# LoRA's products of a two-layer RWKV, conv, MoBA and RetNet trunk: four 32-row tiles or four products over 96 stacked rows

## What is computed

```python
p = p + (token_shift(p) - p) * mu
r, k, v, wl, al = jnp.split(p, [G, 2 * G, 3 * G, 3 * G + L], axis=-1)   # G = 256, L = 32
decay = jnp.exp(-RWKV_DECAY_SCALE * jax.nn.sigmoid(w0 + jnp.tanh(wl) @ w2))
a = jax.nn.sigmoid(a0 + al @ a2)
kk = kk / jnp.maximum(jnp.sqrt(jnp.sum(kk * kk, axis=-1, keepdims=True)), 1e-12)
...
bonus = jnp.sum(rh * kh * r_k.astype(jnp.float32), axis=-1, keepdims=True) * vh
```

## Time and profile before

| | us |
|---|---|
| median of three runs (range) | 576.95 (575.99 to 576.97) |
| the profiled execution: its time | 576.78 |
| its span | 575.0 |
| around the span | 1.78 |

### The profile page before, as it was taken

How to read it: one execution, slowest core, us unless ns; L and a number is a source line. 1 busy time by engine, 2 the same in 40 slices (tenths; PEclk the granted TensorE clock), 3 DMA queues, 4 the chain that set the end, 5 groups by cost and what they waited for, 6 DMA issues and landing times. The chain is left out here.

```text
span 575.0 us, 12739 instructions
## 1 busy us (share of the span) xinstructions
PE 567.4 (99%) x5244; PEld 464.0 (81%) x5244; DVE 381.0 (66%) x644; ACT 278.3 (48%) x555; POOL 249.3 (43%) x197
## 2 busy tenths in 40 slices
PE   9999999999999999999999999999999999999995
PEld 7978888888877777888898788888888777788884
DVE  4999976482488557774543897947537865778163
ACT  5486231343574475534656743324357335735253
POOL 4946552044941323536335455402386313145340
PEclk9999999999999999999999999999999999999998
DMA  9546634056432122353535423332743321224513
GB/s 281 161 130 206 212 97 111 8 130 149 109 79 75 39 75 62 113 171 132 165 117 139 111 77 108 88 70 58 161 127 83 77 73 39 73 75 147 184 40 143
DMA packets 103373, 64.58 MB, mean 112 GB/s; under 512 B 29151, under 2 KB 94227, under 8 KB 103316
## 3 DMA queue, kind: packets, MB, share of 16 engines
q1 hardware_dynamic: 103316, 63.77, 39.4%
HBM read 55.61 MB, written 8.14 MB: 111 GB/s over the span
## 5 line engine op out<-in xcount | busy, mean ns | idle before, releaser
L706 POOL TENSOR_TENSOR w_lo<-w_raw,w_hi 128x512 fp32r<-128x512 f32 x156 | 216.6, 1409 | 283.0 <-ACT w_hi L1295 277.7
L772 PE MATMUL bank<-act_hi,w_hi 128*128 128x512 f32 x432 | 173.2, 401 | 0.0
L775 PE MATMUL bank<-act_lo,w_hi 128*128 128x512 f32 x432 | 168.5, 390 | 0.0
L774 PE MATMUL bank<-act_hi,w_lo 128*128 128x512 f32 x416 | 162.3, 390 | 0.0
L1295 ACT ACTIVATE w_hi<-w_raw 128x512 fp32r<-128x512 f32 x140 | 80.3, 622 | 74.1 <-PE bank L857 28.2
L772 PEld LDWEIGHTS bank<-act_hi,w_hi 128*128 128x128 f32 x432 | 81.1, 188 | 24.7 <-issue 8.2
L775 PEld LDWEIGHTS bank<-act_lo,w_hi 128*128 128x128 f32 x432 | 81.1, 188 | 17.4
L774 PEld LDWEIGHTS bank<-act_hi,w_lo 128*128 128x128 f32 x416 | 78.2, 188 | 14.8
L1221 PE MATMUL bank<-w_hi,act_hi 128*128 128x512 f32 x128 | 50.0, 390 | 0.0
L1223 PE MATMUL bank<-w_hi,act_lo 128*128 128x512 f32 x128 | 49.8, 389 | 0.0
L1222 PE MATMUL bank<-w_lo,act_hi 128*128 128x512 f32 x128 | 49.8, 389 | 0.0
(11 more groups left out here) (217 smaller groups left out, 961.0 us busy)
## 6 DMA issues: line engine op xcount, KB each, us to landing
w_raw<-in_w_in_dram SPq DMA_DIRECT2D x62, 512.0 KB, 4.1
w_raw<-in_w_out_dram SPq DMA_DIRECT2D x16, 512.0 KB, 3.8
pages<-in_x_dram SPq DMA_DIRECT2D x4, 512.0 KB, 6.3
x_or_y<-in_x_dram SPq DMA_DIRECT2D x4, 512.0 KB, 4.2
x_scratch<-x_or_y SPq DMA_DIRECT2D x4, 512.0 KB, 2.9
x_or_y<-x_scratch SPq DMA_DIRECT2D x4, 512.0 KB, 3.7
out_dram<-pages SPq DMA_DIRECT2D x8, 256.0 KB, 2.2
bias_scratch<-pages SPq DMA_DIRECT2D x1, 1280.0 KB, 8.1
```

Source lines behind the costliest of these rows:

```text
L706: ins = pool.tensor_tensor(low, raw, w_hi[:, i % HI, k, 0:n].bitcast(F32), ALU.subtract)
L772: mm(b[:, :], hi, act_hi[:, k, :], start=n == 0, stop=False)
L774: mm(b[:, :], lo, act_hi[:, k, :], start=False, stop=False)
L775: ins = mm(b[:, :], hi, act_lo[:, k, :], start=False, stop=n == KT - 1)
```

## The change

LoRA's products take 96 rows: rows 0 to 31 the high part of the weight, rows 32 to 63 its low part, rows 64 to 95 the high part again, against the input's high part twice and its low part. One float32r product of 96 rows then holds all three terms. The weights are loaded raw three times, ACT copies them all and DVE subtracts for the 32 rows of the low part, in layer 0 only. ACT makes the input's high parts (four copies of 32 rows, one Tanh), and DVE two low parts in a new step `lora_low`, ahead of the scaling that is split off `kk_unit` as `kk_scale`. On PE the products come behind v0 instead of ahead of it. The split of the bonus input becomes a step `rkv_parts` behind the copy of rq0, and bonus's products move behind rk0. At the start six filler products go, and DVE waits for the norm's spread products one at a time, ahead of the first two scalings.

```diff
-          ("kk_norm",), ("kk_unit", 0), ("lora_tanh",), ("shift", "r1"), ("kk_unit", 1), ("lora",), ("shift", "v0"), ("decay_scan",), ("shift", "v1"),
+          ("kk_norm",), ("kk_unit", 0), ("lora_tanh",), ("lora_low",), ("shift", "r1"), ("kk_scale", 0), ("kk_unit", 1), ("kk_scale", 1), ("shift", "v0"), ("lora",), ("decay_scan",), ("shift", "v1"),
...
-    s += [("copy", "rq0"), ("copy", "rq1"), ("bonus",), ("rotate", "rq0"),
-          ("copy", "rk0"), ("rotate", "rq1"), ("scores", 0), ("scores", 1), ("copy", "rk1"), ("rotate", "rk0"), ("to_rows", "v"), ("scores", 2),
+    s += [("copy", "rq0"), ("rkv_parts",), ("copy", "rq1"), ("rotate", "rq0"),
+          ("copy", "rk0"), ("rotate", "rq1"), ("bonus",), ("scores", 0), ("scores", 1), ("copy", "rk1"), ("rotate", "rk0"), ("to_rows", "v"), ("scores", 2),
...
-            for p in range(2):
-                for r, w in ((2 * p, rwkv_w2), (2 * p + 1, rwkv_a2)):
-                    load(lora_w[r * LORA:(r + 1) * LORA], w[:, :, p * P:(p + 1) * P].rearrange("l k c -> k l c"), "const_b")
+            for r in range(3):
+                for z, w in enumerate((rwkv_w2, rwkv_a2)):
+                    load(lora_raw[r * LORA:(r + 1) * LORA, z], w.rearrange("l k c -> k l c"), "lora_loaded")
...
-            idle(3)
             pe.wait_ge(s("const_a"), 16)
             turn(0, 0)
             turn(1, 0)
-            idle(4)
+            idle(1)
...
                 def lora():
-                    pe.wait_ge(*at("lora_in", layer))
-                    for p in range(2):
-                        for z, r0 in (("zw", 2 * p * LORA), ("za", (2 * p + 1) * LORA)):
-                            b = begin(f"{z}{p}", layer)
-                            end(mm(b[:, :], lora_w[r0:r0 + LORA, layer, :], WA[r0:r0 + LORA, :], start=True, stop=True, tile_position=(r0, 0)), f"{z}{p}", layer)
+                    if layer == 0:
+                        pe.wait_ge(s("lora_weight"), 2)
+                    for p in range(2):
+                        for z, name in enumerate(("zw", "za")):
+                            pe.wait_ge(*at("lora_in", layer, 2 - z))
+                            b = begin(f"{name}{p}", layer)
+                            end(mm(b[:, :], lora_w[:, z, layer, p * P:(p + 1) * P], stat_hi[0:3 * LORA, z, :], start=True, stop=True), f"{name}{p}", layer)
...
+                    if layer == 0:
+                        act.wait_ge(s("lora_loaded"), 16 * 6)
+                        go(lora_w.rearrange("p z l c -> p (z l c)"), lora_raw.rearrange("p z l c -> p (z l c)"), ACT.Copy).then_inc(s("lora_weight"), 1)
...
-                    go(WA[2 * LORA:4 * LORA], WA[0:2 * LORA], ACT.Copy).then_inc(s("lora_copied"), 1)
-                    act.wait_ge(*at("lora_copied", layer))
-                    for r0 in (0, 2 * LORA):
-                        go(WA[r0:r0 + LORA], WA[r0:r0 + LORA], ACT.Tanh).then_inc(s("lora_in"), 1)
+                    go(WA[0:LORA], WA[0:LORA], ACT.Tanh).then_inc(s("lora_bent"), 1)
+                    for z in (1, 0):
+                        if z == 0:
+                            act.wait_ge(*at("lora_bent", layer))
+                        for r in range(2):
+                            go(stat_hi[r * LORA:(r + 1) * LORA, z, :], WA[z * LORA:(z + 1) * LORA], ACT.Copy).then_inc(s("lora_high"), 1)
...
             dve.memset(bias_rows[:, :, T:DIST], MASKED)
-            for a in range(2):
-                dve.wait_ge(*full(f"nw{a}", -1))
             for two in (0, 2):
                 for t in (two, two + 1):
                     invert_root(t, 0)
                     for a in range(2):
+                        if t == 0:
+                            dve.wait_ge(*full(f"nw{a}", -1))
...
                         if layer == 0:
+                            dve.wait_ge(s("lora_weight"), 1)
+                            low = slice(LORA, 2 * LORA)
+                            tt(lora_w[low], lora_raw[low], lora_w[low].bitcast(F32), ALU.subtract).then_inc(s("lora_weight"), 1)
                             bias_runs(3)
...
+
+                def kk_scale(p):
                     stt(KN[:, p, :], K[:, p, :], par[:, layer, KKP + p:KKP + p + 1], KN[:, p, :], ALU.mult, ALU.mult).then_inc(s("kk_unit"), 1)
+
+                def lora_low():
+                    for z in (1, 0):
+                        dve.wait_ge(*at("lora_high", layer, 4 - 2 * z))
+                        r = slice(z * LORA, (z + 1) * LORA)
+                        tt(stat_hi[2 * LORA:3 * LORA, z, :], WA[r], stat_hi[r, z, :].bitcast(F32), ALU.subtract).then_inc(s("lora_in"), 1)
```

## The result

The changed kernel takes 579.12 us (median of six runs, 578.87 to 579.3), the kernel before 576.88 (six runs, 575.99 to 577.3). The ratio is 1.0037, 95% interval 1.0027 to 1.0048: slower by 2.2 us, where 578.2 and slower was forecast, with a range of 576.0 to 580.0. The profiled execution took 578.87, with a span of 577.1: 2.1 more than before on either count.

A forecast was written before the change was run, and what follows sets the result against it. PE, busy 99% of the span, was taken as the bound, with VectorE following closely in layer 0. Layer 0's +1.5 and layer 1's -0.1 gave +1.4 on 576.78, so 578.2 us, range 576.0 to 580.0.

The forecast's parts named there:

- PE's own work: LoRA's four products on PE: 96-row products start 0.23 us apart, 0.91 in all, saving 0.37 us in each layer.
- The case without saving: LoRA on PE: a 96-row product costs 0.32 us, so layer 1 gives back nothing, 578.4 us; chance 0.05.
- The start: Kernel start, fewer fillers and earlier first scaling: at most some 0.4 us gained, 0.3 taken, worthless if PE later waits for VectorE.
- The late rise after 13 us: Kernel start: PE's granted clock rising only after 13 us would show that the start lost.
- The rival that the pauses bring the clock down: PE after pauses at LoRA and gate 0: half speed for some microseconds, 579.5 to 581 with the stall; clock chance 0.08.
- steps 1 and 2: Layer 0: ScalarE's weight copy, 1.0 us, delays nothing; VectorE's weights' low part, 1.1 us, makes r0's reading 1.3 us later.
- Step 3: Layer 0, ScalarE's four input copies: 0.60 us each (0.54 to 0.66), tile 7's high part starting at 42.6 instead of 41.57.
- Steps 4 and 5: Layer 0: VectorE's low inputs end at 48.2, PE waits at LoRA; v0 read until 55.05, gate 0 1.15 us later.
- Step 6: Layer 0, scans to gate 1: VectorE's lag 3.0 us, gate 1 read until 71.75, rq1 at 71.85; layer 0 +1.5.
- the rule of turns: VectorE instructions on SBUF alone and GpSimd subtractions never overlap; whoever asked first goes first; each further exchange costs 1.2 us.
- Layer 1: Layer 1: 0.1 to 0.3 of PE's 0.37 us saving is lost, giving -0.1 us, between -0.37 and +0.2.
- No queueing: Layer 0: GpSimd's subtractions fall beside reciprocals, v0 read by 53.5, only PE's work counts, 575.7 us; chance 0.25.

The follow-up runs named there:

- order0_bias: Changed kernel; layer 0's VectorE shifts v0 before the second maximum, reads gate 1 before factors part 1; last eight bias copies on ScalarE behind v0: 576.15 us.
- start_alone: Kernel before with only the change's start: fewer filler products, VectorE waiting for the norm's products one at a time: 576.24 us, ratio 0.9996.
- tile7_first: Changed kernel with ScalarE's high part of tile 7 ahead of the four copies of LoRA's inputs, both layers: 577.52 us, ratio 1.0018.
- v0_first: Changed kernel with VectorE's shift of v0 ahead of the second half's maximum and reciprocal, both layers: 578.24 us, ratio 1.0029.

## Why the prediction was right, and which terms were mis-sized

**PE's own work.** Confirmed: four starts in 0.93 us (328.65 to 329.58), against 0.91 forecast and 1.28 before, 0.36 a layer. The case without saving is out.

**The start.** I took 0.3, which is no more than the scatter of the start. In the changed kernel's trace r0 begins 0.14 us sooner (29.91 against 30.04, first product), but one trace doesn't settle it. Over the traces of this study r0 begins between 29.33 and 30.17 in the eleven with the new start (mean 29.66) and between 29.77 and 30.04 in the three with the old (mean 29.93): 0.3, within a scatter as wide. The timed run of it alone gives 0.2, not told from nothing. As forecast it is swallowed later.

**The clock.** Here the start did suffer in this one trace. PE's timeline of the changed kernel, then of order0_bias, whose start is the same code (each product has 256 columns):

```profile
12.20 0.42 PE L819 MATMUL bank<-act_hi,w_lo 128*128 128x256 f32 x1
12.41 0.41 PE L820 MATMUL bank<-act_lo,w_hi 128*128 128x256 f32 x1
...
13.79 0.28 PE L819 MATMUL bank<-act_hi,w_lo 128*128 128x256 f32 x1
13.91 0.28 PE L820 MATMUL bank<-act_lo,w_hi 128*128 128x256 f32 x1
```

```profile
12.12 0.28 PE L819 MATMUL bank<-act_hi,w_lo 128*128 128x256 f32 x1
12.23 0.28 PE L820 MATMUL bank<-act_lo,w_hi 128*128 128x256 f32 x1
```

The products stand 0.21 apart until 13.3 and 0.12 from then on: 256 columns in 0.21 us are 1.2 a nanosecond, the level of 1.2 GHz, and 0.12 us is near what 2.4 GHz makes of it (the windows view lists a granted clock of 1.00 for this stretch in either trace, so it is read from the products); in order0_bias they stand 0.12 apart from 12.1. So the step comes at another time in another execution of the same start. Six products at 0.09 more cost 0.5 us. Whether the new start makes a late step likelier stays open: three or more slow products stand in five of the eleven traces that have it, and in none of the three with the old one. The late rise after 13 us, my sign for a start that lost, did come. What it costs is small by start_alone, whose trace shows the step as late (13.5) and which isn't slower. The Trainium skill ("TensorE: Matmul & The Clock Gate", Part 1) says that the number of slow products at the start differs from run to run of one kernel. These traces agree, with one to seven slow products over the eleven with this start; that the edit has no part in it they don't show. The rival that the pauses bring the clock down is out: behind the gap of 1.78 us the products stand 0.23 apart as ahead of it (55.74 to 55.97).

**Layer 0, steps 1 and 2.** r0 was to be read at 40.35 and was at 40.31. The way there was another, and that the end came out within 0.04 says nothing for the order laid out: the weights' low part came behind GpSimd's first subtraction instead of ahead of it (2.22 us from 36.50), and the bias copies shrank to 1.65. Both ways give the same sum.

**Step 3** was mis-sized at its dear end: four copies in 2.60, 0.65 each (I took 0.60 and had 0.66 as the end; the cheap end, 0.54, was misread, since half of L1295's pair of 1.15 is 0.58), so tile 7's high part began at 43.0 instead of 42.6. That is the end for which I had +2.6 for layer 0, and +2.80 is what came. Tile7_first shows that tile 7's place behind the copies is worth 1.1 us, though not through the low inputs as this step had it.

**Steps 4 and 5.** The low inputs took 44.8 to 47.3 instead of 45.8 to 48.2, so PE lost 0.3 before LoRA instead of the 1.1 that I had. v0 was read until 55.29 (forecast 55.05) and gate 0 began at 55.44 (55.15).

**Step 6** is the term that failed most: gate 1 read until 72.99, not 71.75, rq1 at 73.14, not 71.85. The lag at gate 1 was 4.2 us and not 3.0, one turn more; 1.56 of it arose behind v0's reading, where 0.56 was forecast. Against the kernel before, the scans are longer by 2.04, L1769 by 1.09 and L1757 by 1.10, and other instructions shorter, L1775 by 0.96, the two of L1765 together by 1.25 and L1745 by 0.44: turns that fell elsewhere before. In v0_first and tile7_first, with the same instructions, the stretch is 1.3 and 1.7 us shorter: which turns fall here hangs on what stands a dozen instructions ahead. So the rule of turns was right, and the layout by hand did not tell which instructions would meet.

**Beside other work.** The weights' copy took 1.05 us on ScalarE and made nobody wait in the changed kernel, as forecast; in v0_first's trace VectorE waits 0.17 us for the ScalarE step behind it, so there was little room. Bonus costs nothing, as forecast; the loads show no wait, but weren't tried apart.

**Layer 1.** -0.1 forecast; from the start of wa in layer 1 to the last product PE is 0.19 faster (its lag behind the kernel before is 2.29 us there and 2.10 at the end). Right, and so is the way: gate 1 is read until 351.27, which with that stage's lag of 1.94 taken off is 349.3, against 349.2 forecast.

**The sum.** +1.5 - 0.1 was forecast; it was +2.8 in layer 0, -0.5 between 80 and 300 us (the stall at 130 us that no edit of these explains), -0.2 in layer 1: +2.1. That the traces differ by 0.7 more than forecast and not by 1.2 is luck: the stall stood in the one trace of the kernel before, and no term of mine had it. With 1.2 the time would still lie within the range. Of the places that I had named, r0's and v0's shift came within 0.15 us (40.31 for 40.3, 54.55 for 54.4), layer 1 without a gap over 0.31, as said; of the gaps, LoRA's was smaller (0.51 for 1.3) and those at gate 0 (1.78 for 0.5) and rq1 (1.28 for 0.4) larger.

**The rivals.** "No queueing" fails by its own condition: v0 was read until 55.29 and not by 53.5, and the kernel is slower. "No saving" fails by the four starts, and the clock by the spacing behind the pauses. The Trainium skill ("SBUF — State Buffer", "Who interferes with whom") says in its list that an instruction of VectorE with at most one input in SBUF lets GpSimd through, if it isn't in a mode that uses both ports, and that one with two contends with it. The traces agree: reciprocal and shifts never lengthen, products, subtractions and scans of two SBUF operands do, by about 1.1 us, and so do copies and the maximum (0.42 and 1.51), which by that list have such modes.

What stays open: 0.4 us of PE in small pieces within v1, gate 0 and gate 1, and which of the turns in layer 0 a given order will bring.

## What to carry to other kernels

Work that is put beside a saturated PE is free only up to the slack of the buffer that its engine hands back; here that was 1.4 and 1.6 us, and 2.3 us were added (1.1 and twice 0.6, turns not counted). When an engine lags, look first at the order of its instructions: two bank readings moved ahead of arithmetic whose result wasn't wanted yet gave back the whole loss with no work removed, but in the layer where VectorE did not lag the same order made PE wait at the scores, so an order belongs to a layer and not to the kernel. And a subtraction on GpSimd is not beside VectorE: put it where VectorE runs reciprocals or reads banks.

## What the runs showed that I had not expected

An idle GpSimd is no free place. An instruction of 2.50 us in its idle time cost VectorE 2.2 us and PE 1.86, and the kernel lost 1.6 us by a move that was to unload VectorE.

Taking work from VectorE gave back about half of it: 2.2 us gave 0.9, 2.5 gave 1.2, 1.65 gave 0.9, each uncertain by 0.8, because other instructions then met the same subtractions.

The place of one ScalarE step, 1.15 us of tile 7's high part, ahead of or behind four copies of 2.60 us, changed the kernel by 1.1 us (ratio 1.0037 to 1.0018, with runs that scatter over 3.5 us), though ScalarE is busy 49% of the span and PE's waits name only VectorE.
